# Gates spread by one float32r product of 256 columns per token, summed by VectorE, in 48 steps from tile 40 on instead of from tile 72 on

## The reference

```python
    top, pos = lax.top_k(cand, PEER_TOPK)
    eidx = jnp.take_along_axis(cidx, pos, axis=-1)
    g = jax.nn.softmax(top, axis=-1)
    u = expert_u[eidx]
    act = jax.nn.gelu(jnp.einsum("td,thkd->thk", xt, u), approximate=False)
    w = (act.astype(jnp.float32) * g).astype(xt.dtype)
    return jnp.einsum("thk,thkd->td", w, expert_v[eidx])
```

## Time and profile before

| | |
|---|---|
| time, median of 3 runs | 1584.78 us (1583.85 to 1585.18) |
| the profiled execution's own time | 1583.63 us |
| its span, first to last instruction | 1581.9 us |
| mean granted TensorE clock | 0.997 |
| busy share of the span | PE 98%, PEld 88%, DVE 73%, POOL 68%, ACT 39% |

### The profile page before, as it was taken

One profiled execution on the slowest core, in us unless ns is written; L12 is line 12 of the kernel. 1 busy time (PEld: TensorE's weight loads), 2 busy tenths in 40 slices (PEclk: granted clock), 3 DMA queues, 4 the chain that ended last, 5 costly groups with the idle time before them and its releaser, 6 DMA issues.

```text
span 1581.9 us, 24953 instructions
## 1 busy us (share of the span) xinstructions
PE 1547.8 (98%) x8645; PEld 1392.6 (88%) x8645; DVE 1151.7 (73%) x2385; ACT 620.3 (39%) x936; POOL 1078.4 (68%) x566
## 2 busy tenths in 40 slices
PE   7999999999899999999999999999999999999998
PEld 6987887788899999999999999888888888888886
DVE  6868564688989953289999993586877676776846
ACT  3223772201333333356665654333333333333331
POOL 5444313444488899898766665788788878878763
PEclk9999999999999999999999999999999999999999
DMA  5211313321499999899999997899999999999961
GB/s 209 96 62 72 107 54 121 125 91 56 144 330 328 313 339 330 293 328 340 356 362 341 354 347 230 320 367 361 359 351 363 360 366 341 350 341 350 340 229 53
DMA packets 168229, 418.37 MB, mean 264 GB/s; under 512 B 15952, under 2 KB 90576, under 8 KB 163296
## 3 DMA queue, kind: packets, MB, share of 16 engines
q1 hardware_dynamic: 124944, 253.92, 45.5%
q0 software_dynamic: 39168, 142.62, 25.0%
q10 hardware_dynamic: 4048, 21.01, 3.4%
HBM read 364.98 MB, written 52.51 MB: 264 GB/s over the span
## 4 chain that ended last, share of the span: by engine, by line
PE 65%; DVE 5%; issue 1%; POOL 1%; DMA 0%; ACT 0%; POOLq 0%; DVEq 0%
PE psum L1611 33%; PE psum L377 8%; PE psum L373 8%; PE psum L374 8%; PE psum L1595 5%; POOL u_lo L1511 1%; PE psum L227 1%; PE psum L218 1%; PE psum L228 1%; DVE h L1791 1%; DVE s_gtile L1858 1%; DVE psum L1862 1%; DVE s_gtile L1860 1%; DVE s_late_rows L1791 1%; DMA h<-in_u_rows,s_u_row 0%
## 5 line engine op out<-in xcount | busy, mean ns | idle before, releaser
L1511 POOL TENSOR_TENSOR u_lo<-u_raw,u_hi 128x1024 fp32r<-128x1024 f32 x220 | 554.7, 2522 | 174.0 <-ACT u_hi L1670 170.1
L1670 ACT CAST u_hi<-u_raw 128x1024 fp32r<-128x1024 f32 x252 | 263.7, 1048 | 304.0 <-PE psum L1611 270.8
L373 PE MATMUL psum<-hn_hi,u_hi 128*128 128x368 f32 x1024 | 341.7, 334 | 5.0 <-ACT s_acts L1675 5.0
L374 PE MATMUL psum<-hn_lo,u_hi 128*128 128x368 f32 x1024 | 337.1, 329 | 0.0
L1611 PE MATMUL psum<-u_hi,s_whi 128*128 128x512 f32 x768 | 298.0, 389 | 0.9 <-ACT s_acts L1675 0.9
L1611 PE MATMUL psum<-u_lo,s_whi 128*128 128x512 f32 x768 | 298.0, 389 | 0.0
L1611 PE MATMUL psum<-u_hi,s_wlo 128*128 128x512 f32 x768 | 297.9, 389 | 0.0
L373 PEld LDWEIGHTS psum<-hn_hi,u_hi 128*128 128x128 f32 x1024 | 193.0, 188 | 5.3 <-issue 5.3
L374 PEld LDWEIGHTS psum<-hn_lo,u_hi 128*128 128x128 f32 x1024 | 193.0, 188 | 0.0
L377 PE MATMUL psum<-hn_hi,u_lo 128*128 128x368 f32 x1024 | 191.5, 329 | 0.7 <-POOL u_lo L1511 0.7
L1544 POOL DMA_INDIRECT s_vrows<-in_v_t,s_v_row x128 | 164.6, 1286 | 26.8 <-issue 25.1
(11 more groups left out here) (329 smaller groups left out, 2687.3 us busy)
## 6 DMA issues: line engine op xcount, KB each, us to landing
u_raw<-in_u_t SPq DMA_DIRECT2D x128, 512.0 KB
u_raw<-in_v_t SPq DMA_DIRECT2D x128, 512.0 KB
act_scratch<-s_acts SPq DMA_DIRECT2D x128, 192.0 KB
scores<-act_scratch SPq DMA_DIRECT2D x32, 768.0 KB
gate_scratch<-s_gtile ACTq DMA_DIRECT2D x10, 2048.0 KB, 9.7
scores<-gate_scratch SPq DMA_DIRECT2D x32, 640.0 KB
m_w_raw<-in_w_in SPq DMA_DIRECT2D x11, 1024.0 KB, 4.8
m_w_raw<-in_w_q SPq DMA_DIRECT2D x8, 1024.0 KB, 4.8
```

The costliest lines, as they stand in the source:

```text
L373: pe.matmul(out, hi[:, d * P:(d + 1) * P], dense(hn_hi, d), start=(d == 0), stop=False)
L374: pe.matmul(out, hi[:, d * P:(d + 1) * P], dense(hn_lo, d), start=False, stop=False)
L1511: pool.tensor_tensor(lo[:, s, :], raw[:, s, :], hi[:, s, :].bitcast(F32), ALU.subtract).then_inc(lo_ready[s], 1)
L1670: act.copy(hi[:, s, :], raw[:, s, :]).then_inc(hi_ready[s], 1)
```

## The change

The change has six parts. The spread is made of one float32r product per token, with one one-hot matrix as weights and 256 moving columns: the other one-hot times the rounded gate (part 0) and times the rest of the gate (part 1). VectorE makes both one-hots of 8 tokens in one operation of 2048 elements with both inputs in SBUF, ACT makes the two weighted copies by 16 small activations, and VectorE adds the two halves with `tensor_reduce` into `gtile`. The spread begins at tile 40, and 24 steps are laid over 40 tiles (one, two, two tiles between steps). The softmax and the turning move from tile 67 and 70 to 35 and 38. The gathers follow one line of 5 per 4 tiles. In the first part, the key scores of list f - 1 stand in the middle of the product f, and the gelus of tiles 0 and 1 ahead of the barrier.

```diff
-LOOP_A = 72
-EXP_AT, TURN_AT = 64, 68
+LOOP_A, LOOP_STEPS, LOOP_TILES = 40, 24, 40
+EXP_AT, TURN_AT = 32, 36
-DOTS_T, DOTS_M, DOTS_J = (0, 8, 10, 10), 12, 12
-DOTS_FREE = 32
+DOTS_T, DOTS_M, DOTS_J = (0, 8, 10, 10), 12, 50
+DOTS_FREE = 2
...
-                    tile_done(product(pe, out, *sides))
+                    product(pe, out, *sides, blocks=range(DC // 2), closes=False)
                     key_scores(f - 1)
-            key_scores(LISTS - 1)
+                    tile_done(product(pe, out, *sides, blocks=range(DC // 2, DC), opens=False))
...
+            for s in range(2):
+                act.wait_ge(tile_used[s], 1)
+                act.activation(acts[:, s, 0:DS], psum[:, s, 0:DS], ACT.Gelu).then_inc(act_ready[s], 1)
...
-        psG = psum[:, 2:4, :].rearrange("p a (n k) -> p a n k", k=P)
+        psG = [psum[:, b:b + 2, :].rearrange("p b (n a k) -> p (b n) a k", a=2, k=P) for b in (2, 6)]
-        iota_ps = psum[:, 6, DT:512]
...
+        hot = nc.alloc_sbuf_tensor_at("s_hot", [P, 2, STEP_TOK, 3, P], F32R, offset=flat_at)
+        pair_ids = nc.alloc_sbuf_tensor_at("s_pair_ids", [P, 2, DT], F32, offset=flat_at + 27 * KB)
...
             def due(n):
-                if n < EXP_AT:
-                    return max(0, min(2 * (n - FIRST_GATHER + 1), in_a * (n - FIRST_GATHER + 1 + U_AHEAD) // (EXP_AT - FIRST_GATHER), in_a))
-                if n < LOOP_A:
-                    return in_a + 3 + 11 * (n - EXP_AT) // 8
-                return min(PAIRS + XK, in_a + DOTS_PRE + 3 * (n - LOOP_A + 3) // 2)
+                return max(0, min(PAIRS + XK, 2 * (n - FIRST_GATHER + 1), 5 * (n - FIRST_GATHER + 1) // 4 + 5))
...
+            def score_and_spread(j):
+                for k in range(LOOP_STEPS):
+                    for m in range(*SPREAD_TILES[k]):
+                        score((LOOP_TILES // UR) * j + (LOOP_A + m) // UR, m % UR)
                     par = k % 2
-                    pe.wait_ge(spread_ready[par], 4 * j + k // 2 + 1)
+                    pe.wait_ge(spread_ready[par], (LOOP_STEPS // 2) * j + k // 2 + 1)
                     for half in range(2):
-                        reached(pe, gates_copied[half], 8 * j + k)
+                        reached(pe, gates_added[half], LOOP_STEPS * j + k)
                         for n in range(4):
-                            last = pe.matmul(psG[:, half, n, :], onehot[:, par, 0, 4 * half + n, :], onehot[:, par, 1, 4 * half + n, :],
+                            last = pe.matmul(psG[half][:, n, :, :], hot[:, par, 4 * half + n, 0, :], hot[:, par, 4 * half + n, 1:3, :],
                                              start=True, stop=True)
...
+            def weigh_hot(step, part):
+                if part == 0:
+                    act.wait_ge(hot_ready, step + 1)
+                for n in range(STEP_TOK):
+                    ins = act.activation(hot[:, step % 2, n, 1 + part, :], hot[:, step % 2, n, 2, :].bitcast(F32), ACT.Copy,
+                                         scale=col(gates[:, part, :].bitcast(F32), step * STEP_TOK + n))
...
+            def add_gates(step):
+                for half in range(2):
+                    dve.wait_ge(gates_summed[half], step + 1)
+                    dve.tensor_reduce(gtile[:, tile, :, t0 + 4 * half:t0 + 4 * half + 4].rearrange("p i t -> p t i"),
+                                      psG[half].rearrange("p n a k -> p n k a"), AX.X, ALU.add).then_inc(gates_added[half], 1)
...
-                for n in range(STEP_TOK):
-                    dve.tensor_scalar(onehot[:, par, 0, n, :], iota_ps, col(pair[:, 0, :], t0 + n), col(pair[:, 1, :], t0 + n),
-                                      ALU.is_equal, ALU.mult)
-                dve.tensor_tensor(onehot[:, par, 1, :, :], iota3, spread_last(turned[1][:, t0:t0 + STEP_TOK], P), ALU.is_equal)\
-                    .then_inc(spread_ready[par], 1)
+                dve.tensor_tensor(hot[:, par, :, 0:3:2, :], iota.unsqueeze(1).unsqueeze(1).to_broadcast([P, STEP_TOK, 2, P]),
+                                  spread_last(pair_ids[:, :, toks].rearrange("p j n -> p n j"), P), ALU.is_equal).then_inc(hot_ready, 1)
```

More of the change, by code:

```diff
@@ L1455, in _ @@
             load_weights(0, 0, 0)
-            load_scores(turns - 1, 2)
-            load_scores(turns - 1, 3)
+            for s in range(1, UR):
+                load_scores(turns - 1, s)
             for s in range(UR):
@@ L1639, in _ @@
             for half in range(2):
[L1640 removed]
+                pe.wait_ge(gates_added[half], n_spread)
             for s in range(UR - 2, UR):
@@ L1696, in _ @@
                 gelu(n // UR, n % UR)
-            def steps(j, also=None, keep=False):
-                for k in range(8):
-                    tile = k // 4
-                    split(2 * j + (LOOP_A // UR + (k + 2) // UR), (k + 2) % UR)
-                    if k % 4 == 0:
-                        reached(act, gates_stored[tile], 16 * j)
-                    for half in range(2):
-                        act.wait_ge(gates_summed[half], 8 * j + k + 1)
-                        t0 = (k % 4) * STEP_TOK + half * 4
-                        act.copy(gtile[:, tile, :, t0:t0 + 4].rearrange("p i t -> p t i"), psG[:, half, :, :]).then_inc(gates_copied[half], 1)
-                    gelu(2 * j + (LOOP_A // UR + k // UR), k % UR)
-                    if also:
-                        also(k)
-                    if k % 4 == 3 and not keep:
-                        act.wait_ge(gates_copied[1], 8 * j + k + 1)
-                        act.dma_start(gate_dram[2 * j + tile], gtile[:, tile, :, :]).then_inc(gates_stored[tile], 16)
+            def weigh_hot(step, part):
[4 more added lines that the diff above has]
+                                         scale=col(gates[:, part, :].bitcast(F32), step * STEP_TOK + n))
+                if part == 1:
+                    ins.then_inc(spread_ready[step % 2], 1)
@@ new lines, in steps @@
+            def steps(j, also=None):
+                for own in range(8 * j, 8 * j + 8):
+                    loop, k, tile, step = own // LOOP_STEPS, own % LOOP_STEPS, own // 4 % 2, own + 1
+                    first, end = SPREAD_TILES[k]
+                    for m in range(first, end):
+                        at = LOOP_A + LOOP_TILES * loop + m
+                        split((at + 2) // UR, (at + 2) % UR)
+                        if m == first and step < n_spread:
+                            weigh_hot(step, 0)
+                        gelu(at // UR, at % UR)
+                        if m == first and step < n_spread:
+                            weigh_hot(step, 1)
+                    if also:
+                        also(own % 8)
+                    if own % 4 == 1 and 4 < own < n_spread - 8 * (KEPT // 2) + 4:
+                        act.wait_ge(gates_added[1], own - 1)
+                        act.dma_start(gate_dram[own // 4 - 1], gtile[:, 1 - tile, :, :]).then_inc(gates_stored[1 - tile], 16)
@@ L1728, in _ @@
             steps(3, also=take_back)
-            with act.Fori(4, n_body - 1) as j:
+            for j in range(4, n_body - 1):
                 steps(j)
-            steps(n_body - 1, keep=True)
+            steps(n_body - 1)
             with act.Fori(LOOP_C // UR, turns - 1) as it:
```

100 lines of the change are left out of this document (60 added, 40 removed).

## The result

The changed kernel takes 1646.87 us (median of 4 runs, 1640.77 to 1647.07), the kernel before 1584.4. The ratio is 1.0387, with a 95% interval of 1.0372 to 1.0403: 62 us more. The forecast had the sign, at 25 us more, and its range ended at 1621. The profiled execution took 1647.07 us, its span is 1645.3, 63.4 longer than before. All of it lies ahead of the values: the last spread ends at 1035.65 us, and what follows takes 610 us, as before. The 63.4 us are 11.7 up to the end of tile 39 and 51.7 from there to the last spread; the forecast had 7.9 and 17.1.

A forecast was written before the change was run, and what follows sets the result against it. The prediction took POOL, with the lock, to set the loop: 424 us against 365 for PE. Start -3.3, retrieval +11.2 and loop +17.1 made 25.0 us more, 1583.6 to 1608.6 (1610 against the median), range 1551 to 1621.

The forecast's parts named there:

- four sums: Loop, per step: each engine's work added up, POOL 8.8 us, VectorE 8.4, PE 7.61, ScalarE 7.3 at most.
- while POOL is the slowest, this is covered: Loop: ScalarE's wait for the one-hots, ahead of a gelu that PE's tile n + 2 needs, costs nothing.
- POOL in the loop: Tiles 40 to 120: low parts, gathers and lock sum to 424 us on POOL, 17.1 us more than before.
- PE's own price: Loop: a spread's eight products take PE 0.94 us instead of 1.79.
- The start of the second part: Gelus ahead of the barrier shorten PE's wait for tile 0: 3.3 us gained, bounds 2 and 6.4.
- POOL in the retrieval: Tiles 20 to 36: early gathers wait for dots, PE stands still 11.2 us, 7.9 net; bounds 4 and 11.
- The granted clock: Start of the second part: lower clock after 5 us of idling lost 1.4 us; half of it counted as gained.
- The first rival: Loop: the lock costs POOL under 0.68 us a step, PE sets the pace, 1551 us; chance 0.20.
- the one in between: Loop: POOL loses 0.8 to 1.6 us a step to the lock, 1555 to 1596 us; chance 0.20.
- VectorE as the bound: Loop: VectorE's one-hots wait for a low part at each step, 438 us, 1624 in all; chance 0.12.
- its sign: Loop: PE idles before the spread (L1607) on VectorE's sums if VectorE is the bound.
- The transfers: Loop at PE's pace: 131.6 MB in 365 us, 360 GB/s, costing nothing beyond the case where PE sets the pace.

The follow-up runs named there:

- the run with the other order: The changed kernel with VectorE's one-hots of a step ahead of the two reductions, instead of behind them: 1619.93 us.
- with lock, orders, POOL's length and loads all relieved: The changed kernel with one-hots ahead of reductions, gelu ahead of weighing, iota in PSUM, low parts of 512 columns, u tiles loaded by half: 1566.22 us.
- slower gathers: The changed kernel with the gathers of the first 36 tiles asked for at about the rate of the kernel before: 1642.67 us.
- both orders and no lock: The changed kernel with one-hots ahead of the reductions, gelu ahead of the weighing, and the iota in PSUM: 1580.54 us.
- Without the lock: The changed kernel with the iota of the one-hots read from PSUM instead of SBUF, gates of tokens 6 and 7 left out: 1612.24 us.
- start edit alone: The kernel before with only the change's first-part edits: key scores in the middle of a product, gelus 0 and 1 ahead of the barrier: 1579.38 us.
- the short dots: VectorE's loop dots cut to 512 columns, in three runs with one-hots ahead of reductions: as is 1619.55, short low parts 1583.04, no lock and gelu first 1582.11 us.

## Why the forecast was wrong

The sign came out, the size didn't, and the mechanism only in part: the lock is real, but the loop isn't POOL's sum.

- **The step that failed** is the one from four sums to the time of the loop: POOL 8.8, VectorE 8.4, PE 7.61, ScalarE at most 7.3, and the largest was taken as the step. It stands in the sentence on ScalarE's wait for the one-hots, ahead of a gelu: "while POOL is the slowest, this is covered". It wasn't covered. PE waited 53.6 us for these gelus, and a step took 9.56 us. The four are tied in a ring: spread, reductions, one-hots, weighing, gelu, tile, with two buffers for the one-hots and two for the tiles' scores. Two reductions in VectorE's queue ahead of the one-hots, 2.35 us, cost 27 us in all (the run with the other order). With the one-hots ahead, 1 us a step of dots less gave nothing: it is what stands ahead of a link that counted there, and not how much VectorE had to do.
- **POOL in the loop**, +17.1: from the end of tile 39 to the end of the last spread it took 458.6 us, not 424. This is the large miss, 34.6 of the 38.4 us between the forecast's 25 and the 63.4 of the spans. The price of one lock was right, 1.91 us and 1.88 measured; how often it is paid was not. POOL's own part of the 458.6 us, without its 69.7 us of waiting for casts, is 389 and not 424, and the 35 us too much are the lock's: 70 where the forecast had 91.7 + 13.0. So this term was too high by about as much as the ring's waits went above it. That the run with the one-hots ahead has a step of 8.94, beside the forecast's 8.8 for POOL, is luck: POOL's own part of it is 8.4.
- **PE's own price** (0.94 us a spread) held. PE at its own pace would have been 365.1 us from tile 40 to 119. No run reached it; the nearest, with lock, orders, POOL's length and loads all relieved, had a step of 7.91 instead of 7.61.
- **The start of the second part**, -3.3 us: right within its bounds. Alone in the kernel before it gives 3.8 us. In the trace PE starts 410.71 - 407.66 = 3.05 sooner, and with its products at the full rate from the first, tile 2 closes 4.4 us sooner (410.41 us, 414.83 before).
- **POOL in the retrieval**, +11.2, net 7.9 with the start: measured 16.1, net 11.7. The mechanism is in the rows: POOL waits 10.9 us for dots (2.75 at q = 16, up to 6.07 later), and PE 9.8 for `u_lo`. What the sum left out is 1.0 for the turning, which was taken out of the loop and not put ahead of it, 1.2 of waiting for a gelu, and some 3.5 of products at the lower clock behind these waits. But it isn't the cause of the loss. With slower gathers the first one-hots and the first spread stand where they were, and 0 to 4 us are gained. The term that I should have had is VectorE's: its first one-hots start at 575.6 us and take 4.71 us with the lock, then come 16 activations in 4.79, against a PE that was ready at 581.
- **The granted clock**: 0.93 from tile 39 to the last spread, where it was 1.00 before. I had the lower clock behind a wait in the earlier trace rows and priced it at the start alone; in the loop it took some 23 us beside the 64 of standing still. With both orders and no lock 15 us of standing still and 6 of slow products are left between the first and the last spread. With the order of VectorE alone it is 32 and 21: the waits halve there, and the clock's share hardly falls.
- **The rivals.** The first rival said that without the lock's cost PE sets the loop, 1551 us. Without the lock the kernel takes 1612 us, and with both orders as well 1580.5, no faster than its start edit alone (1579.4). By the lock's measured price, 70 us with the late dots, 1.2 us a step without the 13.0 forecast for these, the case would have been the one in between, 1555 to 1596; the time was 1647, so it was the ring that none of the cases had. VectorE as the bound had the nearest time, 1624, but its sign, PE idle before the spread on VectorE's sums, is 6.1 us in the changed kernel, and the short dots speak against it. The transfers, costed at nothing, gave up to 11 us once the engines let PE run.
- The Trainium skill ("SBUF — State Buffer", section "SBUF: two separate sides") states that two SBUF inputs of VectorE exclude a GpSimd operation that reads SBUF. The trace agrees for the low part (one-hots of 4.09 us behind it instead of 2.28). The gather's issue was held too, for 1.88 us, and with the iota in PSUM it took 1.04 again. The prediction set this against the sentence; but the gather takes its ids from SBUF (`s_u_row`), so the sentence can cover it, and no run here tells by which access it is held.

## What to carry to other kernels

Where several engines feed each other through two buffers and their sums lie close together (here 7.3 to 8.8 us), the largest sum is no forecast of the step (9.56 here): write down the ring, with what stands ahead of each link in its engine's queue, and ask what the order alone costs. The order in which an engine takes its own work (one-hots ahead of reductions, 27 us) can be worth nearly as much as a lock (35 us), and it costs no work. A lock is paid only where the two operations meet: count how often, here at some 30 of 101 gathers and not at each step. Before moving work from PE to an operation of VectorE with two SBUF inputs, look what GpSimd does beside it, and keep one input in PSUM if there is room; here there was none, and the runs with the iota in PSUM left out the gates of two tokens in eight.

## What I had not expected of the hardware

- An operation of VectorE with two SBUF inputs holds back the issue of an indirect gather as well: 2.92 us instead of 1.04 behind one-hots of 2.28. The kernel before showed it at a dot; here 30 gathers of the loop took over 2.5 us, and none did with the iota in PSUM (the longest took 2.00).
- A reduction of 512 elements of PSUM to 512 takes 1.11 us, one of 1024 to 512 takes 1.22. Its length hardly follows its input here; the dot's does, 0.68 us for 512 and 1.21 for 1024.
- The same 2.06 us of PE standing still was followed by the upper clock in the changed kernel's profile (products of 0.33 us) and by the lower one in that of the start edit alone (0.51 us for 3 us).
